# The experts' products in plain fp32: raw weights, 32-row strips of the array, blocks of 96 tokens

## The reference, cut to what matters

```python
def moe_ffn(h, router_w, router_b, w_up, b_up, w_down, b_down):
    logits = (tok @ router_w + router_b).astype(jnp.float32)     # tok (512, 1024), 32 experts
    top_vals, top_idx = lax.top_k(logits, TOP_K)                 # TOP_K = 4
    gate_w = jax.nn.softmax(top_vals, axis=-1)
    ...
    gu = lax.ragged_dot(x_sorted, w_up, group_sizes) + b_up[e_sorted]      # w_up (32, 1024, 2048)
    g = jnp.minimum(g, SWIGLU_LIMIT)
    u = jnp.clip(u, -SWIGLU_LIMIT, SWIGLU_LIMIT)
    act = (u + 1.0) * (g * jax.nn.sigmoid(SWIGLU_ALPHA * g))
    out = lax.ragged_dot(act, w_down, group_sizes) + b_down[e_sorted]      # w_down (32, 1024, 1024)
    out = out * gate_w.reshape(-1)[order][:, None].astype(out.dtype)
    y = jax.ops.segment_sum(out, token_of, num_segments=n_tok)
```

## Time and profile before

| | us |
|---|---|
| median of 3 runs | 2124.9 (2122.92 to 2125.91) |
| the profiled execution | 2124.89 |
| its span | 2123.0 |
| busy share of the span: TensorE matmul, weight load, VectorE, ScalarE | 96%, 78%, 78%, 61% |

### The profile page before, as it was taken

One profiled execution on the slowest core, in us unless ns is written; L12 is line 12 of the kernel. 1 busy time (PEld: TensorE's weight loads), 2 busy tenths in 40 slices (PEclk: granted clock), 3 DMA queues, 4 the chain that ended last, 5 costly groups with the idle time before them and its releaser, 6 DMA issues.

```text
span 2123.0 us, 30982 instructions
## 1 busy us (share of the span) xinstructions
PE 2037.5 (96%) x9738; PEld 1655.5 (78%) x9738; DVE 1664.4 (78%) x1831; ACT 1305.2 (61%) x1484; POOL 125.0 (6%) x130
## 2 busy tenths in 40 slices
PE   6999999999999998699999999999999999999978
PEld 4777878888888887578888888888888888888746
DVE  4677778888654443589999999999999999999955
ACT  3444354354453321278888888888888888888844
POOL 2000000100100000000000000000000000000031
PEclk9999999999999998699999999999999999999989
DMA  7222222222224342689999999999999999999572
GB/s 263 80 71 59 75 81 64 59 69 61 68 70 139 110 132 97 234 333 383 387 386 383 385 387 385 389 381 388 386 385 384 389 381 389 381 389 383 219 265 82
DMA packets 243401, 528.18 MB, mean 249 GB/s; under 512 B 19789, under 2 KB 128406, under 8 KB 243350
## 3 DMA queue, kind: packets, MB, share of 16 engines
q1 hardware_dynamic: 227696, 474.93, 61.3%
q0 software_dynamic: 6912, 25.17, 3.6%
q10 hardware_dynamic: 8742, 27.40, 3.2%
HBM read 498.01 MB, written 29.43 MB: 248 GB/s over the span
## 4 chain that ended last, share of the span: by engine, by line
PE 90%; DVE 4%; ACT 2%; DMA 2%; issue 1%; ACTq 0%; POOL 0%; DVEq 0%; POOLq 0%
PE psum L1846 85%; PE psum L2176 2%; PE psum L2168 2%; DMA arena<-in_w_in 1%; DVE residual L1788 1%; DVE arena L1326 1%; DVE arena L1233 0%; PE psum L1908 0%; DVE w_lo L1208 0%; DMA y_dram<-arena 0%; PE psum L2016 0%; PE psum L1853 0%; DMA arena<-y_dram,rows_u 0%; ACT arena L774 0%; PE psum L1976 0%
## 5 line engine op out<-in xcount | busy, mean ns | idle before, releaser
L1719 DVE TENSOR_TENSOR h_lo<-arena,h_hi 128x1024 fp32r<-128x1024 f32 x768 | 909.2, 1222 | 93.8 <-ACT h_hi L1095 57.3
L1095 ACT ACTIVATE h_hi<-arena 128x1024 fp32r<-128x1024 f32 x768 | 805.1, 1060 | 213.2 <-PE psum L1846 189.9
L1846 PE MATMUL psum<-h_hi,w_hi 128*128 128x512 f32 x2176 | 864.8, 397 | 8.0 <-DVE w_lo L1208 3.2
L1846 PE MATMUL psum<-h_hi,w_lo 128*128 128x512 f32 x2176 | 850.2, 391 | 0.0
L1846 PE MATMUL psum<-h_lo,w_hi 128*128 128x512 f32 x2176 | 849.9, 391 | 0.0
L1846 PEld LDWEIGHTS psum<-h_hi,w_hi 128*128 128x128 f32 x2176 | 410.3, 189 | 103.0 <-issue 9.2
L1846 PEld LDWEIGHTS psum<-h_hi,w_lo 128*128 128x128 f32 x2176 | 409.7, 188 | 87.0
L1846 PEld LDWEIGHTS psum<-h_lo,w_hi 128*128 128x128 f32 x2176 | 410.4, 189 | 83.8 <-issue 2.9
L1208 DVE TENSOR_TENSOR w_lo<-arena,w_hi 128x1024 fp32r<-128x1024 f32 x104 | 135.6, 1305 | 190.9 <-ACT w_hi L790 189.9
L790 ACT ACTIVATE w_hi<-arena 128x1024 fp32r<-128x1024 f32 x104 | 109.6, 1055 | 98.3 <-PE psum L1846 90.9
L1846 PE MATMUL psum<-arena 128*128 128x64 f32 (+6 forms) x752 | 136.6, 361 | 21.6 <-DVE arena L1687 9.7
(11 more groups left out here) (314 smaller groups left out, 1813.1 us busy)
## 6 DMA issues: line engine op xcount, KB each, us to landing
arena<-in_w_up SPq DMA_DIRECT2D x512, 512.0 KB, 8.0
arena<-in_w_down SPq DMA_DIRECT2D x256, 512.0 KB, 6.8
arena<-in_w_in SPq DMA_DIRECT2D x80, 512.0 KB, 3.9
y_dram<-arena ACTq DMA_DIRECT2D x32, 512.0 KB, 8.6
arena<-in_w_ssd_branch SPq DMA_DIRECT2D x16, 512.0 KB, 3.8
y_dram<-arena ACTq DMA_DIRECT2D x1, 7680.0 KB, 24.3
arena<-in_w_attn_branch SPq DMA_DIRECT2D x8, 512.0 KB, 3.6
arena<-in_w_out SPq DMA_DIRECT2D x8, 512.0 KB, 4.3
```

What stands on the lines that cost most here:

```text
L1095: act.activation(piece_hi[slot], rows, ACT.Copy).then_inc(piece_hi_ready, 1)
L1719: dve.tensor_tensor(piece_lo[slot], rows, piece_hi[slot].bitcast(F32), ALU.subtract).then_inc(piece_lo_ready, 1)
L1846: return pe.matmul(o, l, r, start=start, stop=stop)
```

## The change

The three fp32r products of split operands become one plain fp32 product of the raw ones. Its output is not 128 rows high, but a strip of 32; the four strips of the array take different work:

- A block holds 96 tokens (`CAP`), three strips of 32. There may be 21 extra blocks instead of 15, taken where an expert has more than 96 tokens; the `If` stays.
- Of the 1024 hidden (and of the 1024 output) columns the strips 0, 1 and 2 compute the first 768, each for its own 32 tokens. Strip 3 computes the last 256 columns for all three groups of tokens, one after the other.
- `up` is, for each of 8 k tiles, three groups of four products of 128x32 by 128x512 (256 gate columns and 256 of the other half together), into banks 0 to 2. `down` is, for each k, three of 512, two of 256, three of 256, one of 256 columns, into banks 3 to 5. 12 and 9 bias products follow.
- The pieces need no splitting. `split_piece`, `split_act` and `split_x` are gone; VectorE copies the turned tokens (`copy_x`), ScalarE the turned activations (`copy_act`). Loads wait for the products that used the buffer (`up_used`, `down_used`), TensorE for the landing itself.
- `hidden` is 128 x 768 (the fourth strip's rows hold the last quarter), so 6 transposes turn it, not 8. The tokens are turned by 8 transposes of 96 columns.
- The output leaves PSUM in two copies (96 x 768 and 32 x 768) and two stores. The gate isn't applied there, but where the output rows are added to the residual: one multiply-add with `gate_of` for the add. `gate_tab` and its part of `block_hot` go; the placing of tokens gets a `quotient` for blocks of 96.
- `take_u` waits for `sig_ready`, ScalarE's read of the same bank.

```diff
+CAP, STRIP, STRIPS, QUARTER = 96, 32, 3, 256
+WIDE = STRIPS * QUARTER
+EXTRA = (SEQ * TOPK - TOPK) // CAP
...
             def load_up(i, expert, start=0, end=UP_PIECES):
                 for n in range(start, end):
-                    if not isinstance(i, int) or i:
-                        wait_up_lo(sp, i - 1, n)
+                    if n % 2 == 0 and (not isinstance(i, int) or i):
+                        sp.wait_ge(up_used, KT * (i - 1) + n // 2 + 1)
...
             def expert_out(b):
                 act.wait_ge(down_done, b + 1)
-                wait(act, y_stored, 16 * b)
-                act.activation(y_out, psum[:, 4 * 512:6 * 512], ACT.Copy, scale=gate_tab[:, ds(b, 1)]
-                               ).then_inc(y_ready, 1)
+                wait(act, y_stored, 32 * b)
+                act.activation(y_out[0:CAP], psum[0:CAP, 4 * 512:4 * 512 + WIDE], ACT.Copy).then_inc(y_ready, 1)
+                act.activation(y_out[CAP:P].rearrange("p (s n) -> p s n", s=STRIPS),
+                               psum[CAP:P, 3 * 512:6 * 512].rearrange("p (s n) -> p s n", s=STRIPS)[:, :, 0:QUARTER],
+                               ACT.Copy).then_inc(y_ready, 1)
...
+            def copy_x(b):
+                dve.wait_ge(x_turned, b + 1)
+                dve.tensor_copy(x_T, turned_x).then_inc(x_copied, 1)
...
-            def piece(slot, k, l_hi, l_lo, b):
-                for n in range(2):
-                    ins = mm3(bank(b + n), l_hi[:, k, :], l_lo[:, k, :], piece_hi[slot][:, n, :],
-                              piece_lo[slot][:, n, :], k == 0, False)
...
+            def up(b):
+                pe.wait_ge(x_copied, b + 1)
+                wait(pe, u_ready, b)
                 for k in range(KT):
+                    pe.wait_ge(w_up_landed[k], 32 * (b + 1))
...
+                    for r in range(STRIPS):
+                        for j in range(STRIPS):
+                            mm(bank(r)[strip(j)], x_T[:, k, strip(j)], up_both[k][:, :, r * QUARTER:(r + 1) * QUARTER],
+                               k == 0, False)
+                        ins = mm(bank(r)[strip(STRIPS)], x_T[:, k, strip(r)], up_both[k][:, :, WIDE:FF], k == 0, False)
+                    ins.then_inc(up_used, 1)
...
             def down(i):
+                pe.wait_ge(act_copied, i + 1)
+                wait(pe, y_ready, 2 * i)
                 for k in range(KT):
+                    pe.wait_ge(w_dn_landed[k // 2], 32 * (i + 1))
...
+                    for j in range(STRIPS):
+                        mm(bank(4)[strip(j)], act_strip(k, j), w[:, 0:512], k == 0, False)
+                    for j in range(2):
+                        mm(bank(3 + j, QUARTER)[strip(STRIPS)], act_strip(k, j), w[:, WIDE:D], k == 0, False)
+                    for j in range(STRIPS):
+                        mm(bank(5, QUARTER)[strip(j)], act_strip(k, j), w[:, 512:WIDE], k == 0, False)
+                    ins = mm(bank(5, QUARTER)[strip(STRIPS)], act_strip(k, 2), w[:, WIDE:D], k == 0, False)
+                    ins.then_inc(down_used, 1)
```

More of the change, by code:

```diff
@@ L1092, in split_piece @@
-            def split_piece(number, slot, rows):
-                wait(act, piece_used, number - 3)
-                act.activation(piece_hi[slot], rows, ACT.Copy).then_inc(piece_hi_ready, 1)
-            def split_up(b, start, end):
-                for i in range(start, end):
-                    if i % 2 == 0:
-                        act.wait_ge(w_up_landed[i // 2], 32 * (b + 1))
-                    split_piece(up_piece(b, i), i % 4, up_rows[i])
-            def split_down(b, start, end):
-                for k in range(start, end):
-                    if k % 2 == 0:
-                        act.wait_ge(w_dn_landed[k // 2], 32 * (b + 1))
-                    split_piece(down_piece(b, k), k % 4, down_rows[k])
@@ L1118, in round_of @@
+            def round_of(b):
+                copy_act(b - 1)
+                expert_out(b - 2)
                 swish(b)
-                if not last:
-                    split_x(b + 1)
-                split_down(b - 1, 4, 8)
             def experts(first, end):
-                split_up(first, 0, 4)
-                split_x(first)
-                split_up(first, 4, 16)
                 swish(first)
-                split_x(first + 1)
-                round_of(first + 1, first=True)
-                with act.Fori(first + 2, end - 1) as b:
+                copy_act(first)
+                swish(first + 1)
+                with act.Fori(first + 2, end) as b:
@@ L1131, in experts @@
                     round_of(b)
-                round_of(end - 1, last=True)
-                split_down(end - 1, 0, 4)
-                split_act(end - 1)
+                copy_act(end - 1)
                 expert_out(end - 2)
-                split_down(end - 1, 4, 8)
                 expert_out(end - 1)
@@ L2209, in down @@
+                for j in range(2):
+                    mm(bank(3 + j, QUARTER)[strip(STRIPS)], ones_bf[0:32, strip(STRIPS)], bias_dn[0:32, WIDE:D], False, True)
+                ins = mm(bank(5, QUARTER)[strip(STRIPS)], ones_bf[32:64, strip(STRIPS)], bias_dn[32:64, QUARTER:2 * QUARTER],
+                         False, True)
                 ins.then_inc(down_done, 1)
```

290 lines of the change are left out of this document (112 added, 178 removed).

## The result

The kernel after the change takes **2077.3 us** (median of 4, 2073.85 to 2078.97) against 2124.0 beside it (2122.92 to 2125.91): ratio 0.978, 95% interval 0.977 to 0.979, 46.7 us less. The forecast was 2070, range 2040 to 2150. The profiled execution took 2073.85 us, 51.0 less than the profiled one of before, and has a span of 2072.1 us, 50.9 less; the forecast's sum was -54.8. That the sum comes so near is partly luck: the thirty rounds gained 7 us more than forecast, and a stage that the forecast left at nothing lost 11.

What follows compares the result with a forecast made beforehand. TensorE was taken to bound the kernel, with VectorE 8% behind and DMA about full. The terms -49.5 (thirty rounds), -3.5, -1.25, -1.0 and +0.5 sum to -54.8, from 2124.89 to 2070 us; the range 2040 to 2150 held 0.80.

Steps and rivals of the forecast that it cites:

- The products: Expert rounds on TensorE: four strips run at once, 72 passes a block at 0.433 us, 31.2 us.
- Rival 1: Expert products: strips go two at a time, a block costs 61.8 us instead of 31.2, kernel 3050 us; chance 0.10.
- The rest of a round: TensorE outside the products: `turn_x` 0.85, `turn_act` 0.64, biases 0.73, starts, ends and changes 0.4 us.
- DMA at nothing: Expert rounds: 32.0 to 34.6 us of transfers a block, 25 us of reserve; costed at nothing, up to 30 us in range.
- rival 3: Expert rounds: DMA becomes the bound at 35.2 us a block, kernel 2075 to 2105 us; chance 0.11.
- Ahead of the experts: Before the first block: placing tokens trades VectorE and TensorE work, 0 in sum, bounds -1.5 and +1.5 us.
- First block: Before the rounds: token copy for split -1.2, `up(0)` -1.1, stretch to `turn_act` -0.8, two transposes -0.4; -3.5 us.
- Last `up` and `down(30)`: After the thirty rounds: the last `up` and `down` go from 33.56 to 32.3 us, -1.25.
- Behind it: From `turn_act(31)` to the end: -1.0 us for turn, copy, `down(31)` and output, +0.5 for the multiply in the add.
- the output's landing stays: Kernel end: the output's landing, 8.01 us among 6 MB of late loads, was taken as unchanged.
- Clock: Expert rounds: the forecast is wrong at once if granted clock falls below 1.00 inside them.
- Rivals 2 and 4: Expert products: a pass pays hidden costs, 2139 or 2540 us, chance 0.12; or strips don't overlap, 5020 us, 0.03.

## Why the prediction was right, step by step

- **The products, 72 passes at 0.433 us, 31.2.** Inside a stretch a pass is 0.43; with their starts `up`'s products take 20.74 us (21.09 less 0.35 of biases) and `down`'s 10.50 (1515.20 to 1525.70), 31.24 in all. The term is right to 0.1 us. That four column strips run at once, taken over from two row halves, holds. Rival 1 is out in its strict form: products start ahead of an earlier one that waits, else the order of strips would have cost 34 us a round instead of 9.5, and two in a row would have cost more than 0.07. Right.
- **The rest of a round, 2.6 us** (0.85, 0.64, 0.73, 0.4). Mis-sized: it is 2.3. The step that failed is `turn_x`: its 8 transposes were left at 0.85 us though they are narrower now (96 columns), and take 0.66. The 6 of `turn_act` take 0.65 as said, the biases 0.70 instead of 0.73, and the changes between strips and full height 0.3 instead of 0.4. So the round is 33.58 instead of 33.8; over thirty rounds the gain is 56.2 us and not 49.5.
- **DMA at nothing, up to 30 us in the range.** The result is right and the reasoning half so. The 418 GB/s of the earlier trace rows are not the rate of a whole round; the mean of the earlier trace rows, 387, is much nearer to the 393 of the run with a third of `up`, whose round is 34.2 us. The branch "if 34.6 held, thirty rounds would lag by 24 us and the reserve take it" is what happened, with a lag of 20. So rival 3's premise is true and only its end is missing. The reserve was mis-sized: not 25 us but 20 (20.3 in block 2), of which 2 are left in block 30. That it lasted for just these thirty rounds is luck, not foresight. A TensorE faster still gains little, 9 us in all for 12 us less work a round.
- **Ahead of the experts, 0 (placing 0, bounds 1.5).** The placing itself is right (+0.2). The failed step is that nothing before it was costed: of a DMA that the change reshapes, the zero fill, the prediction says nothing. This stage is 11.2 us longer, and the run that mends the fill has a span 12.8 us shorter. It is the largest error of the sum, and no rival held it.
- **First block, -3.5.** Measured -6.2. The first `up` took 22.51 instead of 25.24 (-2.7, said -1.1), and gather and the first transposes, not costed, took 0.4 less each; copy for split (-1.3), the stall to `turn_act` (-0.8) and its 6 transposes instead of 8 (-0.5) are nearly as said.
- **Last `up` and `down(30)`, -1.25.** Measured -1.6. Right.
- **Behind it, -0.5.** Measured +1.7. Two steps failed. The first is that `down(31)` starts earlier by a copy instead of a split. It doesn't, as TensorE's timeline and ScalarE's show:

```profile
1961.22 0.88 PE L2064 MATMUL psum<-ident,arena 128*128 128x128 f32 x6
1964.56 12.25 PE L1735 MATMUL psum<-arena 128*32 128x512 f32 x144 [2.47 <-issue]
```

```profile
1962.84 0.80 ACT L1034 ACTIVATE arena<-psum 96x768 f32<-96x768 f32 x1
1963.66 0.80 ACT L1035 ACTIVATE arena<-psum 32x768 f32<-32x768 f32 x1
```

  By the program `down(31)` waits for `y_ready`, for both output copies of block 30, since it needs their banks; they end at 1964.46, and it starts at 1964.56. The prediction looked for these copies under `up`, and here is no `up` any more. Behind the pause of 2.47 us the granted clock is 0.72 in the mean from 1964 to 1970 (part of it at the lower level, 1.2 GHz), and `down` takes 12.25 us instead of 10.57; the kernel before has a pause of 2.37 us there and the same 0.72 behind it. The first store of the last block is issued 17.6 us behind the end of the last `up` and `down` (1961.34), the only one of before 17.7 us behind it: nearly all of the gain (1.0) is gone. The second is "the output's landing stays": the chain no longer passes there, but through the late loads.

```profile
1962.98 3.47 issue
...
1972.51 13.71 DMA arena<-in_w_ple_proj
...
1986.26 1.98 PE psum L2149 x8
```

  The multiply-add costs 1.30 us instead of 1.24, as said (0.05 more).
- **Clock.** It stayed at 1.00 (2.4 GHz) in the rounds, as the forecast needed.

Rivals 2 and 4 are out: passes are 0.43 us apart, and all four strips run at once.

## What to carry to other kernels

When a product of fewer rows leaves part of the array idle, give the strips different work by turns: here fp32 in four column strips streamed at full rate, 0.43 us for a pass of all four. Follow every DMA whose partition count the change alters, also in stages it does not name: a fill from 96 partitions took 54% longer than one of 5% fewer bytes from 128. Before a faster engine is counted as gain, divide the bytes of a round by the mean rate of a long stretch, not by its best 2 us; if that is above the new round, the gain lives on a reserve, and lasts only as long as the reserve does.

## What the runs showed of the hardware

- With two products of a strip in a row all four strips stay busy (`up` 21.16 us, 21.09 by turns), with three in a row three strips do (30.58). It fits a strip that holds its running product and one more; a common look-ahead of some six products is not excluded by a run of its own.
- 64-wide and 32-wide products of `up` didn't overlap, and each change of width cost 0.13 to 0.14 us. A turn of full-height transposes between strips lost 0.15 us at its two ends together.
- The fill's 4 KB packets from the SBUF took about 159 ns or about 300; with all 128 partitions as source under 1% were slow, with 112 16%, with 96 26%, with 32 97%.
- Full DMA engines moved 387 to 402 GB/s in stretches of 100 us (share 1.02 to 1.03), with TensorE busy for all of the time or for 78% of it.
